# Passage between the attention and the output projection: heads' root, second spread and clearing of the sums moved

## The reference, cut to what matters

```python
o_fox = fox_attention(fq, fk, fv, log_f)         # 8 heads of width 64
o_sb = stick_breaking_attention(sq, sk, sv)      # 8 heads of width 64
o = jnp.concatenate([rmsnorm_2(merge_heads(o_fox), fox_out_g[l]),
                     rmsnorm_2(merge_heads(o_sb), sb_out_g[l])], axis=-1)
x = x + o @ w_out[l]
h = rmsnorm_2(x, ffn_norm_g[l])
u = causal_dwconv(h @ w_up[l], conv_w[l], conv_b[l])
```

## Time and profile before

| | |
|---|---|
| median of the runs | 2609.21 us |
| the profiled execution | 2611.57 us, of which the span of its instructions is 2609.7 us |
| TensorE busy over the span | 2561.5 us (98%) |
| VectorE busy | 1389.8 us (53%) |
| ScalarE, GpSimd busy | 975.4 us (37%), 820.8 us (31%) |
| mean granted TensorE clock | 0.997 of full speed |

### The profile page before, as it was taken

The page is one execution under the profiler, slowest core; times in us unless marked ns, Lnnn a source line. Parts: engine busy times, 40 slices in busy tenths (PEclk is TensorE's granted clock), DMA queues, the critical chain, the costliest instruction groups (busy, mean ns, idle before and its releaser), DMA issues. The chain is left out here.

```text
span 2609.7 us, 32398 instructions
## 1 busy us (share of the span) xinstructions
PE 2561.5 (98%) x12906; PEld 2134.3 (82%) x12906; DVE 1389.8 (53%) x1286; ACT 975.4 (37%) x1377; POOL 820.8 (31%) x339
## 2 busy tenths in 40 slices
PE   8999999999999999999999999999999999999999
PEld 4888888888888888887888888887888888888887
DVE  5864547766666753445736454555854314431454
ACT  3421144444353420124556555654244213321334
POOL 3755543433434345542011101143422222222230
PEclk9999999999999999999999999999999999999999
DMA  8222321212122253341111111140111111111111
GB/s 338 81 88 71 116 71 57 80 54 70 58 72 69 86 188 105 107 148 52 33 41 41 33 41 41 33 161 18 49 48 48 49 48 48 48 49 64 49 57 65
DMA packets 56551, 194.32 MB, mean 74 GB/s; under 512 B 6856, under 2 KB 10824, under 8 KB 55152
## 3 DMA queue, kind: packets, MB, share of 16 engines
q1 hardware_dynamic: 41312, 141.74, 16.4%
q10 hardware_dynamic: 15120, 50.90, 5.5%
HBM read 158.50 MB, written 29.92 MB: 72 GB/s over the span
## 5 line engine op out<-in xcount | busy, mean ns | idle before, releaser
L238 PE MATMUL G<-H_hi,w_hi 128*128 128x512 f32 x1616 | 502.3, 392 | 1.0 <-ACT silu_zB L724 0.7
L269 POOL TENSOR_TENSOR w_lo<-w_raw,w_hi 128x1024 fp32r<-128x1024 f32 x132 | 346.4, 2625 | 491.1 <-ACT w_hi L263 485.3
L238 PE MATMUL G<-H_lo,w_hi 128*128 128x512 f32 x1616 | 497.8, 389 | 0.0
L238 PE MATMUL G<-H_hi,w_lo 128*128 128x512 f32 x1616 | 497.6, 389 | 0.0
L264 POOL TENSOR_TENSOR w_hi<-w_raw,ones 128x1024 fp32r<-128x1024 f32 x75 | 198.4, 2645 | 591.2 <-PE G L238 470.8
L238 PEld LDWEIGHTS G<-H_lo,w_hi 128*128 128x128 f32 x1616 | 303.3, 188 | 63.4
L238 PEld LDWEIGHTS G<-H_hi,w_lo 128*128 128x128 f32 x1616 | 303.3, 188 | 63.3
L238 PEld LDWEIGHTS G<-H_hi,w_hi 128*128 128x128 f32 x1616 | 300.8, 188 | 64.3 <-issue 4.4
L1857 POOL TENSOR_TENSOR w_lo<-w_raw,w_hi 128x1024 fp32r<-128x1024 f32 x24 | 60.2, 2507 | 480.8 <-ACT w_hi L2073 480.8
L1964 PEld LDWEIGHTS G<-att_v,probsT 128*128 128x128 f32 x1152 | 147.9, 193 | 21.7 <-ACT probsT L2102 12.9
L1912 PE MATMUL G<-A_hi,w_hi 128*128 128x512 f32 x368 | 155.9, 424 | 7.3 <-DVE projected L2255 6.5
(11 more groups left out here) (532 smaller groups left out, 4728.1 us busy)
## 6 DMA issues: line engine op xcount, KB each, us to landing
w_raw<-w_in SPq DMA_DIRECT2D x65, 512.0 KB, 3.6
w_raw<-w_up SPq DMA_DIRECT2D x44, 512.0 KB, 3.6
pre_raw<-w_in SPq DMA_DIRECT2D x30, 512.0 KB, 3.7
wm<-w_mod SPq DMA_DIRECT2D x8, 1024.0 KB, 18.4
w_raw<-w_out SPq DMA_DIRECT2D x16, 512.0 KB, 3.7
w_raw<-w_down SPq DMA_DIRECT2D x16, 512.0 KB, 3.6
xT<-xT SPq DMA_DIRECT2D x8, 512.0 KB, 19.1
b_d<-silu_zB ACTq DMA_DIRECT2D x8, 512.0 KB, 2.6
```

The source lines that it names most:

```text
L238: mm = nc.tensor.matmul(dst[:, n * NB:n * NB + c], w[:, k, :], m[:, k, n * NB:n * NB + c], start=first, stop=last)
L269: nc.gpsimd.tensor_tensor(w_lo[:, slot, 0:kt, :], w_raw[:, slot, 0:kt, :], w_hi[:, slot, 0:kt, :].bitcast(F32), ALU.subtract).then_inc(w_r ...
```

## The change

Three things are done.

1. On ScalarE, a root of a single constant column (`warm`) stands right behind the last squares, so the table of the root function is loaded there; the heads' root follows at once, ahead of `outT` and `heads_high`. On VectorE the inverse and both diagonals follow, ahead of `heads_low`.
2. The second spread ("fox spread") goes to S2, the banks of the first one, after ScalarE has copied the first out of them, and no longer to U2. `early(1)`, which writes U2, no longer waits for ScalarE's copy of the second spread.
3. The clearing of the sums in S2, which stood ahead of the loop on VectorE, now stands inside job 0, between "out2 with sb" and "out2 late", after ScalarE's copy of the second spread.

```diff
--- before.py
+++ after.py
@@ -1747,6 +1747,7 @@
         dump = take("squares_made", [P, P])
         rs = take("row_sums", [P, TILES])
         mn = take("row_mins", [P, 2, 1])
+        warm = take("table_loaded", [P, 1])
         ssp = take("square_sums", [P, ROUNDS, TT])
         ss = take("heads_rstd", [P, 2, TT])
         w_in2 = a["w_in_2"]
@@ -2013,9 +2014,7 @@
                     for t in EARLY_TILES:
                         S.wait(pe, "pool", "heads lo", t)
                     S.wait(pe, "dve", "first", STEPS - 1)
-                elif k == 1:
-                    S.wait(pe, "act", "fox spread")
-                else:
+                elif k > 1:
                     S.wait(pe, "dve", "out2 early", k - 2)
                 S.mark("pe", "out2 early", passes((J_OUT2 + k) % 2, A, range(HEADS, KT), E[k % 2]), k)
 
@@ -2036,7 +2035,8 @@
             late(0, [LATE], False, True).then_inc(gemm_done, 1)
             S.wait(pe, "act", "outT", 2 * ROUNDS - 1)
             S.wait(pe, "dve", "fox diagonals")
-            S.mark("pe", "fox spread", over_features(U, bs[:, 1, :]))
+            S.wait(pe, "act", "sb spread")
+            S.mark("pe", "fox spread", over_features(halves_of(S2), bs[:, 1, :]))
             for k in range(1, KT):
                 early(k)
                 S.wait(pe, "dve", "out2 late", k - 1)
@@ -2180,15 +2180,16 @@
                         squares(r - 1, m - 2)
             for part in range(2):
                 squares(ROUNDS - 1, part)
+            act.activation(warm, epsc, ACT.Sqrt)
+            S.wait(act, "dve", "heads squares")
+            S.mark("act", "heads root", act.activation(ss, ss, ACT.Sqrt, scale=2.0 / D, bias=epsc))
             outT(ROUNDS - 1)
             S.wait(act, "act", "outT", 2 * ROUNDS - 1)
             heads_high(LATE, OT)
-            S.wait(act, "dve", "heads squares")
-            S.mark("act", "heads root", act.activation(ss, ss, ACT.Sqrt, scale=2.0 / D, bias=epsc))
             S.wait(act, "pe", "sb spread")
             S.mark("act", "sb spread", act.activation(gs[:, 1, :], S2, ACT.Copy))
             S.wait(act, "pe", "fox spread")
-            S.mark("act", "fox spread", act.activation(gs[:, 0, :], U2, ACT.Copy))
+            S.mark("act", "fox spread", act.activation(gs[:, 0, :], S2, ACT.Copy))
             for k in range(KT):
                 S.wait(act, "dve", "out2 job", k)
                 S.wait(act, "dve", "out2 sum", k - 1)
@@ -2341,15 +2342,13 @@
             out_of(STEPS // 4 - 1)
             S.wait(v, "act", "square", TT * ROUNDS - 1)
             do("heads squares", v.tensor_reduce(ss, ssp.rearrange("p (i x) t -> p x t i", x=2), AX.X, ALU.add))
-            heads_low(LATE, OT)
             S.wait(v, "act", "heads root")
             do("heads rstd", v.reciprocal(ss, ss))
             me("heads rstd")
             for x, name in enumerate(("sb", "fox")):
                 diagonals(name, bs[:, x, :], ss[:, x, :])
+            heads_low(LATE, OT)
             S.wait(v, "act", "sb spread")
-            do("out2 zero", v.memset(S2, 0.0))
-            me("out2 zero")
             S.wait(v, "pe", "fox spread")
             for k in range(KT):
                 if k >= 2:
@@ -2364,6 +2363,7 @@
                 me("out2 with sb", k)
                 if k == 0:
                     S.wait(v, "act", "fox spread")
+                    me(do("out2 zero", v.memset(S2, 0.0)))
                 v.wait_ge(gemm_done, J_OUT2 + k + 1)
                 do("out2 late", v.tensor_tensor(bs[:, 0, :], G[0], gs[:, 0, :], ALU.mult), k)
                 me("out2 late", k)
```

## The result

The changed kernel took 2613.57 us (median of 20 runs, 2611.15 to 2617.56), the kernel before 2609.19 us in the same comparison (20 runs, 2607.04 to 2611.94). The ratio is 1.0017, with a 95% interval of 1.0010 to 1.0023: 4.4 us slower. The forecast was 2613.3 us, 4.1 slower than before. By the bound of 0.2% it is no change; by its interval it is slower.

The account below looks back on a forecast made before the run. TensorE, 98% busy, was taken as the bound; the passage's 1.42 us gain turns into 1.8 lost at the loop's end, plus 0.2 and 2.1: 4.1 us later, 2613.3 us (8 in 10: 2607.6 to 2615.0).

Parts of the forecast that it names:

- The passage: Ahead of late(1): TensorE's waits of 1.15 and 1.21 us go, the clearing joins the path; TensorE 1.42 us ahead.
- the resumption: At late(1): TensorE, resumed after waiting for VectorE, loses 0.11 us.
- The collision at job 1: VectorE's "out2 with sb" (B) comes 0.25 us behind GpSimd's high part, waits, and ends 2.0 us later.
- The first rival: At job 1, "out2 with sb" (B) goes ahead of GpSimd and VectorE catches up: 1.1 us gain, 2608.1; 18%.
- G holds GpSimd: From job 1, VectorE's "x2 normed" (G) makes GpSimd's high part wait, releasing it 0.13 us before its own end.
- the second rival: In the jobs, "x2 normed" (G) does not hold GpSimd; period at most 10.9 us, time 2609.2; 13%.
- The closed loop: Later jobs: VectorE and GpSimd delay each other, each job takes 11.57 us, not 10.88; loss at loop's end 1.8 us.
- The third rival: In some jobs GpSimd precedes "x2 normed" (G), which waits up to 3.4 us; 6 us slower, 2615.3; 12%.
- VectorE's spare time: In the job loop: VectorE has hardly 0.7 us a job beyond its 1.13 us wait for ScalarE's square.
- The tail: First feed-forward product: start 0.2 us later for job 6's low part, last tile waits 2.1 us for job 7's.

Follow-up runs that it names:

- e2: Kernel before with only the second spread in S2, early(1) without its wait and the clearing inside job 0; heads' root stays late: 2615.19 us, ratio 1.0021.
- e5: Kernel before with one more clearing of S2, 1024 columns, in job 0: 2615.43 us, ratio 1.0025.
- e6: Kernel before with one more clearing of S2, 256 columns, in job 0: 2608.58 us, ratio 0.9998.
- f2: Changed kernel with GpSimd's high part of job k + 2's weights waiting for VectorE's "out2 with sb" of job k, all jobs: 2606.19 us, ratio 0.9991.
- e4: Changed kernel with GpSimd's high parts waiting for VectorE's "out2 with sb" one job too late: 2631.15 us, ratio 1.0083.

## Why the prediction was right

- **The passage.** Forecast: both waits go and late(1) starts 1.53 us earlier (1.42 with the resumption). Measured: 1.37, and 1.20 with the resumption, which took 0.17 and not 0.11 (late(1) lasts 5.61 us). One term was too small: I gave the memset 0.04 us on each side, and it starts 0.29 behind B's end (1799.75 to 1800.04). A row of before had that already: its memset starts 0.28 behind the end of ScalarE's copy (1796.13 + 1.03 to 1797.44). The error moved TensorE and VectorE alike, so the collision did not depend on it.
- **The collision at job 1.** Forecast margin 0.25 us, measured 0.19 (0.23 in e2 and e5). The 0.06 are TensorE's resumption: the high part comes 5.86 behind late(1)'s start, I had 5.69 and 0.11. The first rival, "B wins", had 18% and needed just these 0.2 us. That a margin this small held, with one term off by 0.25, was partly luck: that error moved both sides.
- **G holds GpSimd.** The prediction said that no row of before shows this half, and gave 13% to the second rival, that it isn't so. That was an oversight. Early in the same execution of the kernel before, a scalar_tensor_tensor with two SBUF inputs starts 0.04 us ahead of a high part, and the high part takes 3.45 us, so it was free to go at 121.90, 0.14 ahead of VectorE's end at 122.04:

```profile
120.81 1.23 DVE L882 SCALAR_TENSOR_TENSOR c_gf<-c_gf,c_lf 128x1024 f32<-128x1024 f32 x1
...
120.85 3.45 POOL L402 TENSOR_TENSOR w_hi<-pre_raw,ones 128x1024 fp32r<-128x1024 f32 x1 [3.15 <-DMA pre_raw<-w_in]
```

Measured: GpSimd's high part of 3.10 us in job 2 and up to 3.35 later. The Trainium skill's rule in SBUF — State Buffer, section "SBUF: two separate sides", that the one that starts first has the shared pair for its whole instruction, holds here for a scalar_tensor_tensor with two SBUF inputs too, save that the release came some 0.1 us ahead of its end.

- **The closed loop.** Forecast 11.57 us a job. Measured: late(4) to late(7) start 11.56 apart (1836.07, and 1870.76 three jobs on), each 0.54 or 0.55 us later than due (0.38 or 0.39 in the bracket), forecast 0.5 or so. At late(7) the loss is 1.84 us, forecast 1.8. That they agree so well is luck: the forecast adds the 0.11 of late(3)'s resumption (1826.71) to the start of late(7). Start against start it would have been 1.64, and the 0.2 that are missing are those of the passage.
- **The third rival,** G behind GpSimd: G started 0.21 us ahead of it, forecast 0.18. It did not happen.
- **VectorE's spare time** was misread, with no effect on the sum: the prediction says 0.7 us a job beyond the wait for the square. The windows give 70.72 - 61.51 = 9.21 us for 6.5 jobs, 1.42 each, and less 1.13 that is 0.3. In e6 VectorE catches up by that: B comes 10.63 us apart, TensorE needs 10.88.
- **The tail.** Forecast 0.2 for job 6's low part and 2.1 at the last tile. Measured: the product starts at 1876.52, 0.18 later than due by the row ahead of it (1875.89 + 0.45), too little for a bracket. The last tile starts 1.88 later than due and 4.21 later than before, forecast 4.1. To the end of the stretch the loss is 1.84 at late(7), 0.18 and 1.88 for the two waits, and 0.14, 0.17 and 0.13 for three resumptions, 4.34 in all. The forecast left out the resumption of 0.17 at the product's start. It matters little: VectorE's low part sets when the last tile starts, so what TensorE loses ahead of it comes off its wait. The sum is right within 0.3.
- **What e2 adds:** parts 2 and 3 alone are 5.6 us slower, by the same route. The forecast's sum hid that the change has one part that gains 1.4.

## What to carry to other kernels

An engine that is off the critical path still has an order with its neighbours. Before a wait is removed, look at what each engine follows: here GpSimd followed TensorE and VectorE its own queue, so a gain on TensorE alone moved one past the other, and 0.2 us of order cost up to 5.7 us over seven jobs and the product behind them. Where two engines exclude each other, fix their order with a wait (at the right turn of the loop) rather than leave it to a margin. And when runs scatter by 2 us, measure a stretch inside the profiles: here three kernels in which B went first from job 1 on, as before, and TensorE did not wait for VectorE in the loop gave 100.85, 100.87 and 100.88 us, while their medians scattered over 0.6.

## What the runs showed that I had not expected

- The memset of a PSUM pair started 0.29 us behind the instruction that it waited for, where arithmetic starts 0.03 to 0.04 behind; one of 256 columns started 0.13 behind. From the release to its end the large one took 1.20 us, an arithmetic instruction of the same size some 1.26.
- A clearing of 256 columns in VectorE's slack left no trace in the time, although it made GpSimd's high part wait to 3.08 us; GpSimd had the room.
- The profiled executions came to "heads squares" between 1781.74 (f2) and 1787.13 us (e4), a scatter of 5 us over the same unchanged work ahead of it. Its cause was not looked for.
- Weights that come late cost TensorE 2.0 to 2.1 us in each of five jobs in a row (e4), and 7.2 in the first. With two stretches at half the clock behind such waits that makes 22 us for one wrong index. Why the clock fell behind one wait of 2 us and not behind the others, no run here shows.
